# Three pairs of score banks, one bank for turned weights, one for outputs, and layer norm's channel blocks added on VectorE first, in a hybrid encoder layer

## The reference, cut to what matters

```
h = rmsnorm(x, g_mix);  proj = h @ w_in
a_val, a_gate, q, k, v = split(proj)
u = a_val * sigmoid(a_gate)                       # 512 channels
a_out = silu(layernorm(causal_dwconv(u_hist, conv_w, conv_b), ln_g, ln_b))   # width 31
z = einsum(q, k) / sqrt(64)                       # 8 heads x 64
log_keep = where(vis, log_sigmoid(-z), 0)
later = cumsum(log_keep, reverse) - log_keep
w = where(vis, exp(log_sigmoid(z) + later), 0)    # stick-breaking weights
b_out = head_rmsnorm(einsum(w, v), g_sb)
x = x + concat(a_out, b_out) @ w_out
x = x + hier_moe(rmsnorm(x, g_ffn))               # 2 of 32 experts per token
y = rmsnorm(x, g_final)
```

## Time and profile before

| | us |
|---|---|
| median of three runs | 593.93 (593.90 to 594.14) |
| the profiled execution, device time | 592.3 |
| its span of instructions | 590.6 |
| PE busy | 527.3 (89% of the span) |
| DVE, ACT, POOL busy | 281.3, 155.7, 98.3 |
| mean granted clock of PE | 0.945 of 2.4 GHz |

### The profile page before, as it was taken

One profiled execution on the slowest core, in us unless ns is written; L12 is line 12 of the kernel. 1 busy time (PEld: TensorE's weight loads), 2 busy tenths in 40 slices (PEclk: granted clock), 3 DMA queues, 4 the chain that ended last, 5 costly groups with the idle time before them and its releaser, 6 DMA issues.

```text
span 590.6 us, 7920 instructions
## 1 busy us (share of the span) xinstructions
PE 527.3 (89%) x3189; PEld 336.0 (57%) x3190; DVE 281.3 (48%) x481; ACT 155.7 (26%) x267; POOL 98.3 (17%) x120
## 2 busy tenths in 40 slices
PE   6999999999767799899999799899999877988993
PEld 5779999999545568754555654344343322323330
DVE  2862999999687843714266851111112111001157
ACT  4513122223779832710211201111111111101112
POOL 2100000000657702011002111111112111011002
PEclk9999999999779885999999699999999999889997
DMA  8904745301504400069921789999999999999994
GB/s 295 224 3 149 237 150 168 119 1 43 215 1 158 171 1 0 1 213 424 353 98 59 280 319 427 423 419 421 424 426 425 425 422 423 419 418 422 406 348 158
DMA packets 44764, 148.95 MB, mean 252 GB/s; under 512 B 7124, under 2 KB 23532, under 8 KB 36279
## 3 DMA queue, kind: packets, MB, share of 16 engines
q1 hardware_dynamic: 40263, 139.63, 61.2%
q0 software_dynamic: 4464, 8.80, 3.9%
HBM read 136.29 MB, written 19.59 MB: 264 GB/s over the span
## 4 chain that ended last, share of the span: by engine, by line
PE 60%; DMA 20%; DVE 8%; SPq 4%; issue 4%; ACT 3%; POOL 1%; DVEq 0%; POOLq 0%; ACTq 0%
PE ps L945 17%; DMA big<-in_w_expert_out 12%; PE ps L1170 9%; PE ps L1355 8%; PE ps L1380 5%; DMA cw<-h_dram,low 4%; PE ps L910 3%; PE ps L1071 2%; DVE ps L1895 2%; SPq L632 2%; DMA big<-y_dram 2%; PE ps L1336 2%; PE ps L1125 1%; DMA y_dram<-cw,low 1%; PE ps L898 1%
## 5 line engine op out<-in xcount | busy, mean ns | idle before, releaser
L2168 DVE TENSOR_TENSOR low<-low,ps 128x256 f32<-128x256 f32 x16 | 6.7, 421 | 172.0 <-ACT low L1688 172.0
L1355 PE MATMUL ps<-big,low 128*64 128x512 f32 x320 | 85.0, 593 | 3.3 <-issue 2.3
L945 PE MATMUL ps<-cw_r 128*128 128x280 f32 x256 | 72.3, 292 | 0.0
L1835 DVE SCALAR_TENSOR_TENSOR big<-low,cwt,big 128x590 f32<-128x590 f32 x94 | 72.1, 833 | 0.3
L945 PE MATMUL ps<-low_r,cw_r 128*128 128x280 f32 x256 | 72.2, 292 | 0.0
L945 PE MATMUL ps<-cw_r,big_r 128*128 128x280 f32 x256 | 72.1, 291 | 0.0
L1380 PE MATMUL ps<-big,low 128*64 128x512 f32 x160 | 47.0, 629 | 11.6 <-DMA big<-in_w_expert_out 4.8
L1170 PE MATMUL ps<-cw,low 128*128 128x512 f32 x128 | 56.7, 594 | 0.0
L1355 PEld LDWEIGHTS ps<-big,low 128*64 128x64 f32 x320 | 29.8, 137 | 45.6 <-issue 45.5
L736 POOL TENSOR_TENSOR big<-big 128x590 f32<-128x590 f32 x22 | 28.9, 1335 | 114.7 <-DVE big L1835 106.5
L945 PEld LDWEIGHTS ps<-cw_r 128*128 128x128 f32 x256 | 47.2, 188 | 0.4 <-issue 0.4
(11 more groups left out here) (265 smaller groups left out, 829.3 us busy)
## 6 DMA issues: line engine op xcount, KB each, us to landing
big<-in_w_expert_in SPq DMA_DIRECT2D x16, 2048.0 KB, 18.1
big<-in_w_expert_out SPq DMA_DIRECT2D x20, 1024.0 KB, 25.3
big<-in_w_in SPq DMA_DIRECT2D x20, 512.0 KB, 5.1
low<-in_w_expert_out SPq DMA_DIRECT2D x8, 1024.0 KB, 29.8
low<-in_w_expert_in SPq DMA_DIRECT2D x4, 2048.0 KB, 22.3
cw<-in_w_expert_in SPq DMA_DIRECT2D x4, 2048.0 KB, 25.7
low<-in_w_expert_in SPq DMA_DIRECT2D x4, 1536.0 KB, 21.7
big<-in_w_expert_in SPq DMA_DIRECT2D x6, 1024.0 KB, 32.4
```

The source lines that it names most:

```text
L945: return pe.matmul(ps[:, proj_bank(j) + half, 0:PROJ], w[:, k, :], h[:, k, cols], start=first, stop=last, skip_group_check=True)
L1355: mm = pe.matmul(ps[TILE * half:TILE * half + TILE, gu_bank(g), :], xt[:, k, TILE * half:TILE * half + TILE], wi_at(2 * g + half, k), star ...
L1835: ins = dve.scalar_tensor_tensor(conv[:, i, :], u[:, i, j:j + CW], cwt[:, i, j:j + 1], conv[:, i, :], ALU.mult, ALU.add)
```

## The change

- **Score banks.** Three pairs (banks 0 to 5) take turns, so `scores` waits for place q - 3. The four turns of cached keys become entries of `order` between the steps of group 0 and use those pairs; ACT copies one bank of each, DVE the other. The list grows from 27 to 31 places.
- **Turned weights.** One bank (6). Steps of up to 256 keys are turned and copied with both heads at once, longer ones head by head: `turn_weights` part 0, `weigh` of the step before, `turn_weights` part 1. Each part waits until the part before is copied. ACT copies part 0 between the sigmoids of the two heads of its current step (ahead of the products), and part 1 at the end of the place.
- **Outputs.** One bank (7). ACT copies a group's outputs to SBUF at once (`copy_out`) and squares them from there; `heads_normed` then reads and writes SBUF. `turn_out` goes into bank 6: it waits for the copies of all weights turned before it, and the next `turn_weights` waits for `outputs_in`, which now stands ahead of `weights` in DVE's list.
- **Layer norm.** DVE adds the four blocks with one reduction (`summed`) ahead of `mean` and ahead of `variance`; PE then does 2 matmuls in place of 8, and 5 in place of 20. The wait for POOL's taps and for ACT's squares moves from PE's list to DVE's.
- **Spread of products and roots.** `PRODUCTS` and `POOL_TAPS` change. The carry's two semaphores become a count on one that is there already.

The diff, cut to its core (what is left out changes bank names and semaphores alike):

```diff
-POOL_TAPS = (8, 10, 7)
-PRODUCTS = (1, 1, 1, 1, 2, 1, 1, 2, 1, 1, 2, 2, 1, 2, 1, 2, 1, 1, 1, 1)
+POOL_TAPS = (8, 9, 6)
+PRODUCTS = (1,) * 14 + (2, 1, 1, 1, 1, 2, 1, 1, 1, 1)
...
-SQUARE_LAG, MEANS_LAG, NORM_LAG, OUT_LAG = 4, 4, 6, 7
+COPY_LAG, MEANS_LAG, NORM_LAG, OUT_LAG = 4, 4, 6, 7
+Z_SLOTS = 3
+TURN_BANK, O_BANK = 6, 7
...
+
+        ysum = part(21312, COLS)
+        sqsum = part(10240, COLS)
...
-        order = groups[0] + [dict(ko=0)] + groups[1] + [dict(ko=1)] + groups[2] + [dict(ko=2)] + groups[3]
+        order = [entry for n, st in enumerate(groups[0]) for entry in (st, dict(ck=n))] + [dict(ko=0)] + groups[1] + [dict(ko=1)] + groups[2] + [dict(ko=2)] + groups[3]
...
-            st["q"], st["bank"] = q, 2 * ((NQ - 1 - q) % 2)
+            st["q"], st["bank"] = q, 2 * (q % Z_SLOTS)
+        turned = 0
+        for st in steps:
+            st["turns"] = [(0, 1)] if st["n"] <= 256 else [(0,), (1,)]
+            st["turn"] = turned
+            turned += len(st["turns"])
...
+        def turned_before(g):
+
+            return sum(len(st["turns"]) for st in steps if st["q"] + TURN_LAG <= group_end[g] + OUT_LAG)
+
+        for st in steps:
+            st["turned_out"] = sum(end + OUT_LAG < st["q"] + TURN_LAG for end in group_end)
...
+            def turn_ck(st):
+
+                n = st["ck"]
+                if n == 0:
+                    pe.wait_ge(ck_loaded, 16)
+                bank_free(st["q"])
                 for a in range(2):
...
+                        mm = pe.transpose(ps[:, st["bank"] + a, P * i:P * i + P], ckraw[:, b, P * i:P * i + P], ident[:, :])
                 mm.then_inc(ck_turned, 1)
...
-                if q < 2:
...
+                if q < Z_SLOTS:
...
-                gone = order[q - 2]
+                gone = order[q - Z_SLOTS]
...
+                elif "ck" in gone:
+                    for r in range(2):
+                        pe.wait_ge(ckt_ready[r], gone["ck"] + 1)
...
-            def turn_weights(st):
-
-                s, n = st["s"], st["n"]
+            def turn_weights(st, part):
+
+                s, n, t = st["s"], st["n"], st["turn"] + part
                 pe.wait_ge(w_ready, s + 1)
-                if s:
-                    pe.wait_ge(wtt_ready, s)
+                if t:
+                    pe.wait_ge(wtt_ready, t)
                 else:
-                    pe.wait_ge(ckt_ready[0], 2)
+                    pe.wait_ge(qk_done, 8)
+                if part == 0 and st["turned_out"]:
+                    pe.wait_ge(mixb_ready, st["turned_out"])
                 w = wts[s % 4]
-                for a in range(2):
+                for m, a in enumerate(st["turns"][part]):
+                    lo = max(n, P) * m
                     if n < P:
                         p0 = st["p0"]
-                        mm = pe.matmul(ps[p0:p0 + n, 4 + a, 0:P], w[:, a, 0:n], ident[:, :], start=True, stop=True)
+                        mm = pe.matmul(ps[p0:p0 + n, TURN_BANK, lo:lo + P], w[:, a, 0:n], ident[:, :], start=True, stop=True)
                     for b in range(n // P):
-                        mm = pe.transpose(ps[:, 4 + a, P * b:P * b + P], w[:, a, P * b:P * b + P], ident[:, :])
+                        mm = pe.transpose(ps[:, TURN_BANK, lo + P * b:lo + P * b + P], w[:, a, P * b:P * b + P], ident[:, :])
                 mm.then_inc(w_turned, 1)
...
-                pe.wait_ge(wtt_ready, s + 1)
-                if st["first"]:
-                    if g < 2:
-                        pe.wait_ge(ckt_ready[1], 2)
-                    else:
-                        pe.wait_ge(mixb_ready, g - 1)
+                pe.wait_ge(wtt_ready, st["turn"] + len(st["turns"]))
+                if st["first"] and g:
+                    pe.wait_ge(o_copied, g)
...
             def turn_out(g):
 
                 pe.wait_ge(onorm_ready, g + 1)
+                pe.wait_ge(wtt_ready, turned_before(g))
                 if g == 1:
                     for unit in range(2):
-                        mm = pe.transpose(ps[:, O_BANK[g], P * unit:P * unit + P], ot[:, P * unit:P * unit + P], ident[:, :])
+                        mm = pe.transpose(ps[:, TURN_BANK, P * unit:P * unit + P], ot[:, P * unit:P * unit + P], ident[:, :])
                 else:
                     for i in range(NI):
-                        mm = pe.transpose(ps[:, O_BANK[g], P * i:P * i + P], osb[g % 2][:, P * i:P * i + P], ident[:, :])
+                        mm = pe.transpose(ps[:, TURN_BANK, P * i:P * i + P], osb[g % 2][:, P * i:P * i + P], ident[:, :])
                 mm.then_inc(o_turned, 1)
 
...
             def mean(st):
                 bank_free(st["q"])
-                pe.wait_ge(yc_ready, NI)
-                pe.wait_ge(pool_tap_done, NI * TAPS - taps_by_dve)
-                for i in range(NI):
-                    for half in range(2):
-                        mm = pe.matmul(ps[:, st["bank"] + half, 0:HALF], nones[:, :], yc[:, i, HALF * half:HALF * half + HALF],
-                                       start=i == 0, stop=i == NI - 1, skip_group_check=True)
+                pe.wait_ge(sums_ready, 1)
+                for half in range(2):
+                    mm = pe.matmul(ps[:, st["bank"] + half, 0:HALF], nones[:, :], ysum[:, HALF * half:HALF * half + HALF],
+                                   start=True, stop=True)
                 mm.then_inc(mean_done, 1)
...
                 bank_free(st["q"])
-                for i in range(NI):
-                    pe.wait_ge(devsq_ready, i + 1)
-                    for c in range(NC):
-                        lo = min(P * c, COLS - P)
-                        mm = pe.matmul(ps[:, st["bank"], c:c + 1], lnsq[:, i, lo:lo + P], nones[:, 0:1],
-                                       start=i == 0 and c == 0, stop=i == NI - 1, skip_group_check=True)
+                pe.wait_ge(sums_ready, 2)
+                for c in range(NC):
+                    lo = min(P * c, COLS - P)
+                    mm = pe.matmul(ps[:, st["bank"], c:c + 1], sqsum[:, lo:lo + P], nones[:, 0:1],
+                                   start=c == 0, stop=True, skip_group_check=True)
                 mm.then_inc(var_done, 1)
...
+                early, late = step_at(q - TURN_LAG), step_at(q - SUM_LAG)
+                if early:
+                    turn_weights(early, 0)
+                if late:
+                    weigh(late)
+                if early and len(early["turns"]) == 2:
+                    turn_weights(early, 1)
                 if group_at(q - OUT_LAG) is not None:
                     turn_out(group_at(q - OUT_LAG))
...
+            def copy_weights(st, part):
+                s, n, heads = st["s"], st["n"], st["turns"][part]
+                act.wait_ge(w_turned, st["turn"] + part + 1)
+                if part == 0 and s >= 2:
                     act.wait_ge(av_done, s - 1)
                 r = slice(st["p0"], st["p0"] + n) if n < P else slice(0, P)
                 n = max(n, P)
-                act.copy(wtt[s % 2][r, :, 0:n], ps[r, 4:6, 0:n]).then_inc(wtt_ready, 1)
+                act.copy(wtt[s % 2][r, heads[0]:heads[-1] + 1, 0:n],
+                         ps[r, TURN_BANK, 0:n * len(heads)].rearrange("p (a t) -> p a t", a=len(heads))).then_inc(wtt_ready, 1)
...
-            def output_squares(g):
+            def copy_out(g):
 
                 act.wait_ge(av_done, groups[g][-1]["s"] + 1)
+                if g == 0:
+                    act.wait_ge(y_cleared, 16 * 9)
+                if g >= 2:
+                    act.wait_ge(o_turned, g - 1)
+                n = 256 if g == 1 else 512
+                o = ot if g == 1 else osb[g % 2]
+                act.copy(o, ps[:, O_BANK, 0:n]).then_inc(o_copied, 1)
+                act.wait_ge(o_copied, g + 1)
                 if g >= 1:
                     act.wait_ge(onorm_ready, g)
-                n = 256 if g == 1 else 512
-                act.activation(osq[:, 0:n], ps[:, O_BANK[g], 0:n], ACT.Square, scale=HD ** -0.5).then_inc(osq_ready, 1)
+                act.activation(osq[:, 0:n], o, ACT.Square, scale=HD ** -0.5).then_inc(osq_ready, 1)
...
             for q in range(NQ + TURN_LAG):
-                if group_at(q - SQUARE_LAG) is not None:
-                    output_squares(group_at(q - SQUARE_LAG))
-                if step_at(q):
-                    shares(step_at(q))
-                    if q in (0, 1):
-                        copy_ck(2 * q)
+                if group_at(q - COPY_LAG) is not None:
+                    copy_out(group_at(q - COPY_LAG))
+                st, early = step_at(q), step_at(q - TURN_LAG)
+                if st and len(st["turns"]) == 1:
+                    shares(st, (0, 1))
+                elif st:
+                    shares(st, (0,))
                 elif q < NQ and "ko" in order[q]:
                     copy_ko(order[q])
+                elif q < NQ and "ck" in order[q]:
+                    copy_ck(order[q])
+                if early and q < NQ:
+                    copy_weights(early, 0)
```

(36 more changed lines are left out.)

89 lines of the change are left out of this document (34 added, 55 removed).

## The result

The changed kernel took 612.57 us (median of 4 runs, 607.96 to 614.65) against 593.91 for the kernel before (587.23 to 594.14, 4 runs): a ratio of 1.0332, 95% interval 1.0236 to 1.0427. That is 18.7 us slower. The forecast was 596.5, range 590.5 to 600.5: the direction was right, the size was not, and the time lies outside the range. The profiled execution took 614.65, its span 612.9; it is the slowest of the four.

A forecast was written before the change was run, and what follows sets the result against it. The time was taken to be decided by when the output projection's main part begins (257.97 us), after a chain of waits, lastly PE's. Legs of -2.4 + 0.4 + 4.6 = +2.6 on the 593.93 median gave 596.5 us, range 590.5 to 600.5.

The forecast's parts named there:

- leg 1: Stretch to the end of group 2's head sums (203.28 us before): forecast -2.4 us, bounds -3.5 and -1.0.
- leg 3: From the mean's end (213.47) to the output projection's main part (257.97), 44.5 us before: forecast +4.6, bounds +3.4 and +8.
- leg 2: From group 2's head sums (203.28) to the mean's end (213.47), 10.2 us before: forecast +0.4, bounds 0 and +3.4.
- From there ACT sets the pace: From the third cached step ACT bounds attention, giving back 2.3 us of idle time; net 3.4 us gained.
- The hold by POOL: After each root, POOL's tap can hold `heads_normed`, now reading only SBUF, for 1.34 us; the first hold called certain.
- the same operation: Reduction over four blocks ahead of the mean, priced from L1914 (512 elements in 0.68 us): 2.6 us.
- The mean's term: Two of eight matmuls for the mean, 6.67 / 4 = 1.67 us at the lower clock.
- three waits between halves: Behind the variance, three places where nothing covers ACT's copy between halves, about 0.5 us each; +1.4 in all.
- The sums pay: Rival: the wait at `outputs_in` is covered and PE's saved work counts, -5.8, about 588 us (586 to 592.5); 19%.
- The reduction is slow: Rival: reducing across blocks at the scan's price costs 3 us more, twice: 602.5 us; 10%.
- Nothing left over: Rival: leg 1 at best, PE back at 2.4 GHz early: about +0.2, 594 us (592.8 to 595.1); 19%.
- the third pair doesn't free DVE: Ruled out 13.1 us less (583) from DVE's scan waits, since ACT is busy 33.68 of 36 us; folded into first rival.

The follow-up runs named there:

- c0: The changed kernel itself, run again beside the kernel before: ratio 1.0339, profiled execution 608.77 us.
- e5: Changed kernel with POOL_TAPS (8, 9, 8), so all but one tap stand ahead of POOL's root again: ratio 1.0268 to the kernel before.
- e1: Changed kernel with layer norm's sums given back to PE (8 and 20 matmuls): ratio 1.0252 to the kernel before.
- e2: Changed kernel with unused matmuls put into PE's waits ahead of mean, variance and group 2's turn of outputs: ratio 1.0271 to the kernel before.
- e10: Changed kernel with each reduction over four blocks replaced by two additions of halves on DVE: ratio 1.0210 to the kernel before.
- e4: Kernel before the change with only layer norm's two reductions moved to DVE: ratio 1.0104.
- e12: Kernel before the change with layer norm's sums on DVE as additions of halves: ratio 0.9967.
- e9: Changed kernel with sums on PE, taps ahead of root, outputs behind weights, two score pairs and two turn banks (both heads together): ratio 0.9992 to the kernel before.
- e18: Changed kernel with two score pairs, two turn banks (both heads together) and outputs behind weights; reductions and taps kept: ratio 1.0126 to the kernel before.
- e11: Kernel before the change with only ACT's copies of turned weights moved ahead of products and squares: 585.19 us, ratio 0.9888.
- e15: Kernel before the change with copies of turned weights ahead of products and layer norm's sums as additions of halves on DVE: ratio 0.9885.
- e16: e15 with POOL_TAPS (8, 10, 8), all taps ahead of the root: ratio 0.9924 to the kernel before the change.
- e7: Changed kernel with two score pairs and two turn banks, both heads turned and copied together: ratio 1.0202 to the kernel before.
- e14: Changed kernel with two score pairs and two turn banks, weights still turned head by head: ratio 1.0192 to the kernel before.
- e17: Changed kernel with sums on PE, taps ahead of root, two score pairs and two turn banks; outputs still ahead of weights: ratio 1.0050 to the kernel before.
- e13: Changed kernel with two score pairs instead of three, still one turn bank filled head by head: ratio 1.0335 to the kernel before.
- e8: Changed kernel with sums on PE, taps ahead of root, outputs behind weights, second half copied ahead of ACT's squares; pairs and bank kept: ratio 1.0154 to the kernel before.
- e3: Changed kernel with outputs_in moved behind weights in DVE's place: ratio 1.0305 to the kernel before.

## Why the prediction was wrong

Two steps failed: in leg 1 that ACT sets the pace, and in leg 3 that PE's clock behind the variance stays as it was. In c0 the change cost 16.4 us against the 2.6 of the sum; of the 13.8 between them 4.6 lie in leg 1, 2.5 in leg 2 and 7.5 in leg 3, and the rest took 0.8 less.

**Leg 1: the sign was wrong, and the step that failed is "From there ACT sets the pace".** The sum let ACT give back 2.3 us of idle time. ACT became idle for longer instead, 6.1 us in place of 2.3 from 168 to 204, against the earlier trace rows:

```profile
168.00:204.00 36.00, 28.11 (x384) 18.79 (x384) 27.60 (x40) 29.94 (x57) 23.49 (x20) 0.88 0.38 136
```

Most of the added idle time is waiting for turned weights, which the sum had in 1 us together with the holds (ACT from 168 to 206: total, times, longest):

```profile
ACT big L1597 <- PE ps L1079: 4.2, 4, 1.5
```

The 3.72 us ahead of the scan at 187.07 follow a second hold by POOL. The prediction read such a hold off this instruction in the kernel before (L1901, now L1933, the carry's correction), but had a price only for `heads_normed`. L1933 takes 0.16 us elsewhere; here it ends 0.14 us after the first of two taps of 1.31 us:

```profile
179.04 1.27 DVE L1933 TENSOR_TENSOR big<-big,stat 128x2 f32<-128x2 f32 x1
```

```profile
178.86 2.62 POOL L753 TENSOR_TENSOR big<-big 128x590 f32<-128x590 f32 x2 [0.45 <-ACT big L1636]
```

PE's next turn then waits 1.84 us for DVE, and ACT's next copies 1.33 and 0.96 us for PE. c0 and e5 have the same hold and waits of 3.88 and 4.03 us at that scan. In e1, e2 and e10, whose lists are the same up to this point, L1933 takes 0.16 us, and that scan begins 5.7 to 6.2 us after L1933's start in place of 8.0 to 8.4. So the hold goes with some 2 us, but leg 1 does not go by it alone: e2 and e10 are as late without it. Over the profiles leg 1 goes with PE's granted clock from 170 to 190 us: it was 0.90 to 1.00 where the leg ended by 203.4 (before, e4, e12, e1, e9, e18), and 0.74 to 0.90 where it ended after 205 (the changed kernel and its other variants; 0.77 in e2 and e10). Whether a lower clock is a cause or follows from the waits is open.

The copies ahead of the products do gain, 1 to 3 us by the profiles of e11, e15 and e16. The sum had 0.5 us for them at the first cached step.

**The hold by POOL: right.** The tap takes 8.25 / 6 = 1.38 us from 170.16, and `heads_normed` ends 0.61 us after it, about its time of 0.68 where no tap runs. That agrees with the rule of the Trainium skill, page "SBUF — State Buffer", section "Who interferes with whom". e9 keeps this hold (1.92 us) and is level with the kernel before all the same.

**Leg 2: mechanism right, one term mis-sized.** Root to 208.41, taps to 212.96 (4.55 for 4.0), reduction 4.05 for 2.6, mean 2.26 for 1.67, and 0.3 of handovers: 13.2. The largest miss is the reduction, between the two ends that the prediction gave (2.6 and 5.6). The value from "the same operation" was the wrong choice: L1914 reads neighbours. The mean's term was a misreading: four matmuls at 1.2 GHz take 2.26 us, so sixteen would take 9.0, and before's 6.67 us were not all at that clock.

**Leg 3 up to the variance: right.** The first scan begins 10.8 us after the mean (9.8 to 11.5 forecast), the variance ends at 24.2 (21.5 to 23.2 forecast), and the reduction's miss of 1.45 us accounts for the excess.

**Leg 3 behind the variance: the step that failed is PE's clock.** The prediction took before's 25.15 us, and with it before's clock, and added 1.4 for three waits between halves. It took 37.3 us in the profiled execution and 32.2 in c0. The waits were sized about right: there are four, a wait of 1.80 us that PE had before is gone, and PE's idle time grew by 1.4 us (1.9 in c0). The term that failed is the one held fixed, the time that PE is busy. The windows from the end of the variance to the projection's main part, in the kernel before, after and in c0:

```profile
232.82:257.97 25.15, 23.35 (x139) 16.90 (x140) 11.62 (x12) 12.51 (x17) 3.08 (x3) 0.94 0.24 84
```

```profile
243.76:281.05 37.29, 34.06 (x139) 24.85 (x139) 11.83 (x12) 13.10 (x21) 3.08 (x3) 0.63 0.15 57
```

```profile
242.80:274.97 32.17, 28.43 (x138) 19.32 (x138) 11.68 (x12) 13.03 (x21) 3.08 (x3) 0.78 0.18 66
```

The same 139 matmuls (one is missing from c0's record) keep PE busy for 10.7 us longer at 0.63 of 2.4 GHz in place of 0.94, and for 5.1 us longer at 0.78. Why the clock is lower there after the change is open, and no run here moved it alone. It differs between two executions of one kernel (0.63 and 0.78). The single turn bank is not needed for it: e4, e7, e9, e14, e17 and e18, without that bank, have 0.79 to 0.83. Nor do waits for a sum decide it: e1 has none ahead of the variance and 0.79, while e15 waits 6.95 us there and has 0.92.

**The rivals.** "The sums pay" was to be decided by when the copy behind the squares ends: by 3 us after the mean, it said, and it ended 8.9 us after it (228.42). "The reduction is slow" came halfway true, at 4.05 us. "Nothing left over" needed PE back at 2.4 GHz early in leg 3; its mean clock there was 0.63. That the third pair doesn't free DVE is right by e13, but the reason given, ACT's load, is not what the changed kernel shows: ACT was busy for 83% of the time from 168 to 204, where the prediction expected over 90.

## What to carry to other kernels

Here, to split a double buffer into two halves of a single one cost a round trip per half wherever nothing else stood between them, and a further wait for what else used that buffer; look for those places behind every other wait, not only on today's path. Don't price a reduction by another one whose elements lie otherwise, and try additions of halves in its place. An engine that is the bound before a change need not be the bound after it. And where a PE stretch runs at either clock, make the sum at both: here that term alone was 5 to 11 us, more than the forecast's whole change. Before reading a part's effect from one profile, see how far the same lists differ between profiles: in leg 1 it was 3.8 us.

## What the runs showed of the hardware that was not expected

A reduction over four blocks 2304 bytes apart took 4.05 us for 2304 elements, and two additions of halves 1.36 + 0.76 us for the same result.

PE was granted 1.2 GHz from 246 to 262 us while it was busy for 16.00 of the 16 us; ahead of that it had waited 6.96 us for the second reduction. In c0, the same kernel with the same wait, it was granted 0.82 of 2.4 GHz in that window. In e9 the clock fell to 0.51 from 242 to 248 us, where PE was busy for all 6 us as well.

From the variance to the projection the same matmuls took 25.2 to 25.5 us (before, e11, e12, e15, e16), 28.0 to 29.5 (e4, e7, e9, e14, e17, e18), 31.4 to 32.2 (c0, e1, e2, e5, e8, e10, e13), 34.3 (e3) and 37.3 (the changed kernel's first profile), the last nine all with the single turn bank.
